# A gated-DeltaNet projection stage: modulation terms moved from GpSimd to VectorE, two row buffers, convolution ahead of scaling

## What is computed

```python
def adaln(c, w, b, n):
    m = jax.nn.silu(c) @ w + b                     # (1, n * 1024)
    return [t[:, None, :] for t in jnp.split(m, n, axis=-1)]

def gated_deltanet(h, w_in, conv_w, ...):
    proj = h @ w_in                                # 2048 x 4112
    qkv, z, a, b = jnp.split(proj, [...], axis=-1)
    qkv = causal_dwconv_silu(qkv, conv_w)          # 4 taps along the sequence, then silu
    q, k, v = jnp.split(qkv, [A_QK, 2 * A_QK], axis=-1)
    q = l2_norm(q.reshape(bsz, seq, A_HEADS, A_DK))   # x * rsqrt(sum(x * x) + eps), 8 heads of 128
    k = l2_norm(k.reshape(bsz, seq, A_HEADS, A_DK))
    ...
```

## Time and profile before

| What | Value |
|---|---|
| Median of 3 runs | 3215.01 us (3204.41 to 3220.05) |
| Profiled execution, its own time | 3207.62 us |
| Its span in the profile | 3205.9 us |
| TensorE busy over the span | 3039.8 us (95%) |
| VectorE busy | 1735.6 us (54%) |
| ScalarE busy | 1231.2 us (38%) |
| GpSimd busy | 1021.7 us (32%) |
| Chain that ended last, TensorE's share | 55% |
| Mean granted TensorE clock | 0.981 of full speed |

### The profile page before, as it was taken

How to read it: one execution, slowest core, us unless ns; L and a number is a source line. 1 busy time by engine, 2 the same in 40 slices (tenths; PEclk the granted TensorE clock), 3 DMA queues, 4 the chain that set the end, 5 groups by cost and what they waited for, 6 DMA issues and landing times.

```text
span 3205.9 us, 39987 instructions
## 1 busy us (share of the span) xinstructions
PE 3039.8 (95%) x15148; PEld 2288.9 (71%) x15148; DVE 1735.6 (54%) x2711; ACT 1231.2 (38%) x2161; POOL 1021.7 (32%) x692
## 2 busy tenths in 40 slices
PE   6999899999995999799999999999999999999998
PEld 4766667888884888688887888887555555555587
DVE  5555555557564666565422221103877777778643
ACT  4444445544322555343322211120444544445411
POOL 0689870123225454100000000001454545545400
PEclk9999999999997999899999999999999999999999
DMA  5333431576746675566643431116463433331343
GB/s 225 94 119 112 139 107 54 167 230 200 215 132 195 204 241 186 146 184 192 192 103 109 124 100 73 73 54 164 96 139 90 119 85 95 90 90 48 98 138 125
DMA packets 291084, 428.05 MB, mean 134 GB/s; under 512 B 74654, under 2 KB 187942, under 8 KB 285756
## 3 DMA queue, kind: packets, MB, share of 16 engines
q1 hardware_dynamic: 261612, 359.19, 38.0%
q0 software_dynamic: 13168, 50.42, 4.9%
q10 hardware_dynamic: 16112, 15.86, 1.8%
HBM read 274.58 MB, written 150.69 MB: 133 GB/s over the span
## 4 chain that ended last, share of the span: by engine, by line
PE 55%; ACTq 1%; DVE 1%; ACT 1%; issue 1%; POOL 0%; DMA 0%; DVEq 0%; SPq 0%; POOLq 0%
PE at_ps L1872 8%; PE at_ps L1923 5%; PE at_ps L1775 5%; PE at_ps L1910 5%; PE at_ps L1777 5%; PE at_ps L1776 5%; PE at_ps L1854 5%; PE at_ps L1857 4%; PE at_ps L1840 3%; PE at_ps L1788 2%; PE at_ps L1789 2%; PE at_ps L1790 2%; ACTq L2375 1%; PE at_ps L1886 1%; ACT at_probs L2472 1%
## 5 line engine op out<-in xcount | busy, mean ns | idle before, releaser
L2472 ACT ACTIVATE at_probs<-at_ps 128x512 f32<-128x512 f32 (+3 forms) x640 | 331.3, 534 | 338.0 <-PE at_ps L1857 272.5
L2096 DVE TENSOR_REDUCE at_partial<-at_ps 128x1 f32<-128x512 f32 (+3 forms) x640 | 370.9, 605 | 141.4 <-PE at_ps L1840 109.0
L106 PE MATMUL pa_y<-pa_h_high,pa_w_high 128*128 128x512 f32 x992 | 395.1, 398 | 4.8 <-ACT pa_ybuf L811 4.8
L108 PE MATMUL pa_y<-pa_h_high,pa_w_low 128*128 128x512 f32 x992 | 387.0, 390 | 0.0
L107 PE MATMUL pa_y<-pa_h_low,pa_w_high 128*128 128x512 f32 x992 | 386.9, 390 | 0.0
L1552 POOL TENSOR_TENSOR at_plain<-at_plain,at_probs 128x512 f32<-128x512 f32 (+3 forms) x256 | 309.7, 1210 | 224.8 <-ACT at_probs L2472 208.9
L1775 PE MATMUL at_ps<-at_h_high,at_w_high 128*128 128x512 f32 x768 | 299.6, 390 | 1.0 <-DVE at_w_low L2025 0.9
L1777 PE MATMUL at_ps<-at_h_high,at_w_low 128*128 128x512 f32 x768 | 298.8, 389 | 0.0
L1776 PE MATMUL at_ps<-at_h_low,at_w_high 128*128 128x512 f32 x768 | 298.8, 389 | 0.0
L1854 PE MATMUL at_ps<-at_h_low,at_h_high 67*128 67x512 f32 (+3 forms) x640 | 260.3, 407 | 12.1 <-ACT at_probs L2472 11.8
L1857 PE MATMUL at_ps<-at_h_low,at_h_high 128*128 128x512 f32 (+3 forms) x640 | 252.7, 395 | 0.0
(11 more groups left out here) (344 smaller groups left out, 5468.2 us busy)
## 6 DMA issues: line engine op xcount, KB each, us to landing
at_h_low<-s_Q SPq DMA_DIRECT2D x96, 256.0 KB, 7.1
s_qkv<-pa_sil POOLq DMA_DIRECT2D x16, 1024.0 KB, 6.7
pa_sil<-s_qkv SPq DMA_DIRECT2D x16, 1024.0 KB, 6.0
dr_kv<-s_qkv SPq DMA_DIRECT2D x16, 1024.0 KB, 8.6
s_Q<-at_parts SPq DMA_DIRECT2D x64, 256.0 KB, 4.1
at_h_high<-s_K SPq DMA_DIRECT2D x32, 512.0 KB, 5.5
pa_wraw<-in_a_w_in_dram ACTq DMA_DIRECT2D x15, 1024.0 KB, 6.1
pa_gb<-in_b_mod_w_dram SPq DMA_DIRECT2D x24, 512.0 KB, 3.6
```

The source lines that it names most:

```text
L106: nc.tensor.matmul(out, w_high[:, k], h_high[:, k], start=k == 0, stop=False)
L108: ins = nc.tensor.matmul(out, w_low[:, k], h_high[:, k], start=False, stop=k == KC - 1)
L2096: reduced.done(v.tensor_reduce(partial[:, u % 2, h * NQ + sub, grp:grp + 1], rough[:, j % 3, 0:width], AX.X, ALU.max))
L2472: probs_ok.done(a.activation(probs[:, R % 2, t, h, off:BLK], logits[:, l % 3, off:BLK], ACT.Exp))
```

## The change

Four edits, all in `deltanet_projection`:

1. The terms of the later modulations go from GpSimd to VectorE. Each term is one instruction, `macc = mw * csil + macc`, in place of two. They stand at the end of VectorE's work for tile T, four to a tile, T = 0 to 11. GpSimd keeps the clearing of `macc` and the load of the bias (`begin_mod`), and no longer waits for the bias itself; VectorE does.
2. The weights of the terms have three slots in place of two (the third is the tile `X`).
3. Query and key rows use `acc` and `sil` in turn (`rows[T % 2]`). The convolution writes the row, silu runs in place, and the store reads the same buffer. Silu no longer waits for a store; the convolution of tile T waits for the store of row T - 2. Each buffer has a semaphore for its stores.
4. In VectorE's order the convolution of tile T comes before the scaling of tile T - 1.

```diff
+        rows = [acc, sil]
-        junk, mw, macc, mrow = flat_tile(Bd), (xs[2], xs[3]), xs[4], flat_tile(Bd)[0:1]
+        junk, mw, macc, mrow = flat_tile(Bd), (xs[2], xs[3], xs[5]), xs[4], flat_tile(Bd)[0:1]
@@ SyncE
-                sp.dma_start(mw[m % 2], w[...]).then_inc(mw_in[m % 2], 16)
+                sp.dma_start(mw[m % len(mw)], w[...]).then_inc(mw_in[m % len(mw)], 16)
...
-                if m >= 2:
-                    sp.wait_ge(mod_step, m - 1)
+                if m >= len(mw):
+                    sp.wait_ge(mod_step, m - len(mw) + 1)
...
-            sp.wait_ge(stored, 16 * QK)
+            for s in range(2):
+                sp.wait_ge(stored[s], 16 * QK // 2)
@@ GpSimd
-            def later_mod(T):
-                ...
-                for k in range(T % 2 * KC // 2, (T % 2 + 1) * KC // 2):
-                    m = piece * KC + k
-                    pool.wait_ge(mw_in[m % 2], 16 * (m // 2 + 1))
-                    g.tensor_scalar(mw[m % 2], mw[m % 2], csil[:, k:k + 1], None, ALU.mult).then_inc(mod_term, 1)
-                    pool.wait_ge(mod_term, m + 1)
-                    if m:
-                        pool.wait_ge(mod_step, m)
-                    g.tensor_tensor(macc, macc, mw[m % 2], ALU.add).then_inc(mod_step, 1)
+            def begin_mod(piece):
+                if piece == 0:
+                    pool.wait_ge(turned_x, NB * KC)
+                else:
+                    pool.wait_ge(mod_summed, piece)
+                g.memset(macc, 0.0).then_inc(mod_zero, 1)
+                pool.wait_ge(mod_zero, piece + 1)
+                w, b, j = later[piece]
+                pool.dma_start(macc[0:1], b[j * D:(j + 1) * D].unsqueeze(0)).then_inc(mb_in, 16)
             for T in range(QK):
-                if T < 2 * len(later):
-                    later_mod(T)
+                if T % 2 == 0 and T // 2 < len(later):
+                    begin_mod(T // 2)
                 scaled.wait(pool, T)
-                pool.dma_start(s_qkv[:, :, T]..., chunk_major(sil[:, :])).then_inc(stored, 16)
+                pool.dma_start(s_qkv[:, :, T]..., chunk_major(rows[T % 2][:, :])).then_inc(stored[T % 2], 16)
@@ VectorE
             def convolve(T):
-                if T:
+                to = rows[T % 2] if T < QK else acc
+                if T >= QK:
                     silu_done.wait(dve, T - 1)
+                if 2 <= T <= QK:
+                    dve.wait_ge(stored[T % 2], 16 * (T // 2))
...
+            def later_mod(T):
+                if T == 0:
+                    dve.wait_ge(c_ready, 1)
+                if T % 2 == 0:
+                    dve.wait_ge(mb_in, 16 * (T // 2 + 1))
+                for m in range(T * KC // 2, (T + 1) * KC // 2):
+                    dve.wait_ge(mw_in[m % len(mw)], 16 * (m // len(mw) + 1))
+                    if m:
+                        dve.wait_ge(mod_step, m)
+                    v.scalar_tensor_tensor(macc, mw[m % len(mw)], csil[:, m % KC:m % KC + 1], macc, ALU.mult, ALU.add).then_inc(mod_step, 1)
...
                         split_next(T)
-                        if 1 <= T <= QK:
-                            scale(T - 1)
                         if kind(T) != "z":
                             bank_free.wait(dve, T, n)
                             convolve(T)
+                        if 1 <= T <= QK:
+                            scale(T - 1)
+                        if T < 2 * len(later):
+                            later_mod(T)
@@ ScalarE
                     if T < QK:
-                        if T:
-                            act.wait_ge(stored, 16 * T)
-                        silu_done.done(a.activation(sil[:, :], acc[:, :], ACT.Silu))
+                        row = rows[T % 2][:, :]
+                        silu_done.done(a.activation(row, row, ACT.Silu))
                         silu_done.wait(act, T)
                         scaled.wait(act, T - 1)
-                        squared.done(a.activation(sq[:, :], sil[:, :], ACT.Square))
+                        squared.done(a.activation(sq[:, :], row, ACT.Square))
```

More of the change, by code:

```diff
@@ L206, in deltanet_projection @@
             "convolved", "silu_done", "squared", "summed", "rooted", "scaled"))
-        stored, late_stored = st.pool_sem("stored"), st.pool_sem("late_stored")
+        stored, late_stored = [st.pool_sem(f"stored{s}") for s in range(2)], st.pool_sem("late_stored")
         dve_step, act_step = st.sem("dve_step"), st.sem("act_step")
@@ L222, in deltanet_projection @@
             "squared_x", "logged_x", "rooted_x", "scaled_x", "turned_x", "h_scaled", "h_rounded", "h_made"))
-        mw_in = [st.sem(f"mw_in{s}") for s in range(2)]
+        mw_in = [st.sem(f"mw_in{s}") for s in range(len(mw))]
         mb_in, mod_step, mod_summed, mod_copied, mod_stored = (st.sem(n) for n in (
             "mb_in", "mod_step", "mod_summed", "mod_copied", "mod_stored"))
-        mod_zero, mod_term, summed_mod = (st.sem(n) for n in ("mod_zero", "mod_term", "summed_mod"))
+        mod_zero, summed_mod = (st.sem(n) for n in ("mod_zero", "summed_mod"))
         block = st.block()
@@ L388, in begin_batch @@
                                            pattern=[[1, SB], [-1, SB]], channel_multiplier=0))
-            def later_mod(T):
[L392 to L403, removed]
-                for k in range(T % 2 * KC // 2, (T % 2 + 1) * KC // 2):
-                    m = piece * KC + k
-                    pool.wait_ge(mw_in[m % 2], 16 * (m // 2 + 1))
-                    g.tensor_scalar(mw[m % 2], mw[m % 2], csil[:, k:k + 1], None, ALU.mult).then_inc(mod_term, 1)
-                    pool.wait_ge(mod_term, m + 1)
-                    if m:
-                        pool.wait_ge(mod_step, m)
-                    g.tensor_tensor(macc, macc, mw[m % 2], ALU.add).then_inc(mod_step, 1)
+            def begin_mod(piece):
[7 more added lines that the diff above has]
+                pool.dma_start(macc[0:1], b[j * D:(j + 1) * D].unsqueeze(0)).then_inc(mb_in, 16)
             for T in range(QK):
-                if T < 2 * len(later):
-                    later_mod(T)
+                if T % 2 == 0 and T // 2 < len(later):
+                    begin_mod(T // 2)
                 scaled.wait(pool, T)
-                pool.dma_start(s_qkv[:, :, T].rearrange("c p j -> p c j"), chunk_major(sil[:, :])).then_inc(stored, 16)
+                pool.dma_start(s_qkv[:, :, T].rearrange("c p j -> p c j"), chunk_major(rows[T % 2][:, :])).then_inc(stored[T % 2], 16)
             for T in range(QK, TILES + 1):
@@ L581, in convolve @@
                     if j == 0:
-                        steps.did(v.tensor_scalar(acc[:, :], x, w, None, ALU.mult))
+                        steps.did(v.tensor_scalar(to[:, :], x, w, None, ALU.mult))
                         continue
                     steps.wait()
-                    ins = v.scalar_tensor_tensor(acc[:, :], x, w, acc[:, :], ALU.mult, ALU.add)
+                    ins = v.scalar_tensor_tensor(to[:, :], x, w, to[:, :], ALU.mult, ALU.add)
                     steps.did(ins) if j < 3 else convolved.done(ins)
@@ L589, in scale @@
                 rooted.wait(dve, T)
-                scaled.done(v.tensor_tensor(sil[:, :], sil[:, :], sq[:, :], ALU.mult))
+                scaled.done(v.tensor_tensor(rows[T % 2][:, :], rows[T % 2][:, :], sq[:, :], ALU.mult))
+            def later_mod(T):
[8 more added lines that the diff above has]
+                    v.scalar_tensor_tensor(macc, mw[m % len(mw)], csil[:, m % KC:m % KC + 1], macc, ALU.mult, ALU.add).then_inc(mod_step, 1)
             gates = Steps(dve, gates_dve)
@@ L748, in decays @@
                     act.wait_ge(nn_ok, 1)
-                    act.wait_ge(stored, 16 * QK)
+                    for t in range(2):
+                        act.wait_ge(stored[t], 16 * QK // 2)
                 pt_ok.wait(act, c - 1, 1)
```

2 lines of the change are left out of this document (1 added, 1 removed).

## The result

The changed kernel takes 3160.89 us (median; 3155.64 to 3163.69), the kernel before 3215.02 (3204.41 to 3220.05): the ratio is 0.983, with the interval 0.9808 to 0.9852. The profiled execution took 3155.64 us with a span of 3153.9, 52.0 less than the span before.

What follows compares the result with a forecast made beforehand. It took GpSimd's terms, and the single buffer making silu wait behind them, to set the first stage's pace. 47.7 us in the tiles plus 2.3 before them gave 50 off: 3161 us, between 3157.6 and 3165; range 3147 to 3188.

Steps and rivals of the forecast that it cites:

- Pace, and the 50 us: First stage: tiles at 25.3 or 27.5 us; 47.7 us lost in 15 tiles plus 2.3 before them come back.
- The clock comes back with the gaps: TensorE, first stage: without gaps the clock returns to 1.00, so 50.0 us come back and not only 34.2.
- Rival D: TensorE, first stage: the clock stays low though the gaps go; 34 us off, 3174 to 3181; chance 0.07.
- Terms at 1.3 us: VectorE: each fused term takes 1.3 us with the wait between terms, four to a tile 5.2 us.
- What is late is the store.: First stage: ScalarE's silu waited 183.6 us in 15 waits for row stores, issued late behind GpSimd's terms.
- the gates' gap: Gates work in tile 14 leaves ScalarE late for the next banks: 4.8 us of TensorE waiting, expected to go.
- The order and the buffers cost nothing.: Tile slots: convolution first and two buffers cost nothing; 10 us of slack for the square, 8 for the store.
- The slot: Schedule within one tile, counted from its norm burst: convolution until +10.4, scaling +12.7, square +14.7, last term +27.5.
- The third slot makes this fit.: Even slots on VectorE: a third weight slot lets the terms end at +27.5, as the next burst comes.
- Rival C: VectorE's new ring through sum, clearing, bias and terms closes: slower, 3240 at 5 us more a pair; chance 0.03.
- Rivals A and B: First stage: A, part of the stall stays, 17 to 33 us off (0.13); B, pace set elsewhere, 0 to 15 (0.05).

Runs made afterwards that it cites:

- e1: The kernel before with only the two row buffers, terms still on GpSimd and scaling first: 3207.06 us.
- e9: The kernel before with two row buffers and the convolution ahead of scaling, terms still on GpSimd: 3233.03 us.
- e2: The kernel after with one row buffer and scaling first, keeping the terms on VectorE and the third weight slot: 3168.41 us.
- e4: The kernel after with scaling ahead of the convolution again: 3173.29 us.
- e8: The kernel after with one row buffer, the convolution still ahead of scaling: 3226.9 us.
- e3: The kernel after with two weight slots in place of three: 3162.01 us.
- e5: The kernel after with one further VectorE step ahead of each term, leaving the sum as it is: 3169.04 us.
- e6: The kernel after with two further VectorE steps ahead of each term, leaving the sum as it is: 3216.9 us.
- e12: e8 with SyncE's store of the modulation row four weight loads later: 3198.25 us.
- e10: The kernel after with two weight slots and, in tiles 0 to 11, four multiplications and subtractions on GpSimd that nobody needs: 3225.37 us.

## Why the prediction was right, point by point

- **Pace, and the 50 us.** It forecast 392.7 us for 15 tiles, 2.3 before the first burst and the last burst near 516. Measured: 391.1, 3.4, and 512.91. The 1.6 us between are the tiles' own paces, 25.24 and 27.32 against 25.3 and 27.5. The time, 3161 against 3160.89, owes a little to luck: the sum named 50 us, where it is 52.0 from the profiled execution before to the one after, and 54.1 between the medians. From the median the same sum gave 3165.
- **The clock comes back with the gaps.** Idle time alone explained 34.2 us, and 52.7 came; the granted clock is 1.00 without gaps and 0.93 to 0.98 in each kernel that has many. Rival D was wrong. The Trainium skill (TensorE: Matmul & The Clock Gate, HAM oscillation) says that the array falls back to half speed after such a wait; the runs agree, with 52.7 us back for 34.2 idle. Shorter waits can cost as well: the burst at 125.18 is drawn out behind 2.30 us.
- **Terms at 1.3 us.** 1284 ns. Contention was named as a side benefit (2735 to 2352 ns) and costed at nothing, since it lies off the path once the terms are gone. Right for the sum.
- **"What is late is the store."** The step that was incomplete, though the sum did not need it. The store was late, and so were the convolution beside it (1.7 us ahead of the store in the slot of the earlier trace rows, and the releaser in e1) and GpSimd's own ring (9.2 us of waits in e1, 56.3 in e9). The prediction said that the terms "and the single buffer that makes silu wait" set the pace. e2 shows that the single buffer had no part in the 47.7 us but for the gates' gap, once the terms are gone and scaling goes first, and e1 that removing it alone gives nothing that can be measured (tiles 439.2 us against 440.4).
- **"The order and the buffers cost nothing."** Right only as a pair: together they remove the gates' gap (4.8 us idle, 6.5 to 7 in that tile). The buffer without the order gives nothing (e4 against e2); the order without the buffer costs 58 us (e8 against e2). The prediction costed both in one schedule, and did not ask what one needs of the other.
- **The slot.** Forecast and measured: convolution +10.4 and +10.5, scaling +12.7 and +12.7, silu +12.4 and +12.5, square +14.7 and +14.7, bias landed +20.9 and +22.5 (4.9 us from issue to its term), last term +27.5 and +28.9. The next slot starts 1.5 us late, where up to 1 was allowed. The weight loads took 4.8 us in the list of DMA issues, not 3.6.
- **"The third slot makes this fit."** Wrong: with two slots (e3) it fits as well.
- **Rival C.** Its ring exists, with about the slack that was given: 10 us a pair against 9 to 14 by e5 and e6, and 20 us a pair more (e6) lose the 50 us and a little, as was named. Not in the prediction: ScalarE's copy of the summed row, SyncE's queue behind it and the weights as a second way around (e8, e12).
- **Rivals A and B.** No part of the stall stayed, and the changed parts did set the pace.

What stays open: why GpSimd's multiplication takes 3967 ns in e9 and 3584 in e10, and why the rows in `acc` and in `sil` are slowed so differently; the mutual slowing is shown, what sets its size is not. No version was found that beats the kernel after: TensorE is busy in all of 122 to 750 us there.

## What to carry to other kernels

A wait names only the last of several late things: before costing its removal, ask where the next releaser ends, since here taking away the named one (the store) gave nothing that could be measured, and taking away the work behind all of them gave 46 of 54 us. Work of an engine beside VectorE is not free because nobody waits for it: moving 48 terms onto VectorE filled 62 us of its idle time (1.28 each), cost TensorE no wait, and made the kernel 46 us shorter. And when two edits are made together, cost each without the other: the same order that gained 7 us in the tiles with two buffers lost 58 with one.

## What the runs showed of the hardware

GpSimd and VectorE slow each other down by more than the kernel before had shown. A step of the convolution takes 2352 ns alone and 2735 beside the terms. That mean mixes two kinds of slots: three steps take 9.88 us in those where TensorE then stands still for some 5 us (256.48 above), and 7.13 in those between. In e10, where VectorE is busy for 297 of 394 us against 216 before, the mean is 3480 for one row buffer and 2712 for the other; a term of VectorE goes from 1284 to 1847 ns. GpSimd's multiplication goes from 3526 to 3967 in e9. The Trainium skill (SBUF — State Buffer, SBUF: two separate sides) says that the two share a pair of ports and that the loser of a conflict stands still; the sign agrees, and the sizes are those of these runs.
